# Marking the keys of the expert gates with three engines: squared distances on GpSimd, three second keys of sixteen on ScalarE

## What the reference computes

```python
s1, i1 = lax.top_k(s[:, :, 0], PEER_TOPK)
s2, i2 = lax.top_k(s[:, :, 1], PEER_TOPK)
cand_s = s1[..., :, None] + s2[..., None, :]
cand_i = i1[..., :, None] * N_KEYS + i2[..., None, :]
top_s, pos = lax.top_k(cand_s, PEER_TOPK)
idx = take_along_axis(cand_i, pos)            # 128 pairs for each token
gate = softmax(top_s)
act = gelu(einsum('pkd,pd->pk', expert_u[idx], t)) * gate
out = einsum('pk,pkd->pd', act, expert_v[idx])
```

## Time and profile before

| what | value |
|---|---|
| time, median of 3 runs | 5070.51 us (5069.15 to 5071.11) |
| profiled execution: its own time | 5068.12 us |
| its span, first to last instruction | 5066.4 us |
| TensorE / VectorE / ScalarE / GpSimd busy | 78% / 46% / 32% / 3% of the span |
| first scatter, 1339.3 to 1540.4 us | 201.1 us: TensorE 149.7, VectorE 179.9, ScalarE 181.8 busy |
| second scatter, 2991.0 to 3091.7 us | 100.7 us: TensorE 74.4, VectorE 90.0, ScalarE 90.9 busy |
| mean granted TensorE clock | 0.873 (1.0 is 2.4 GHz, 0.5 is 1.2 GHz) |

### The profile page before, as it was taken

How to read it: one execution, slowest core, us unless ns; L and a number is a source line. 1 busy time by engine, 2 the same in 40 slices (tenths; PEclk the granted TensorE clock), 3 DMA queues, 4 the chain that set the end, 5 groups by cost and what they waited for, 6 DMA issues and landing times. The chain is left out here.

```text
span 5066.4 us, 61125 instructions
## 1 busy us (share of the span) xinstructions
PE 3929.2 (78%) x20597; PEld 2743.7 (54%) x20597; DVE 2348.7 (46%) x4852; ACT 1609.3 (32%) x3013; POOL 170.8 (3%) x148
## 2 busy tenths in 40 slices
PE   5988998883376999999968635999846776677766
PEld 2448995342264787778745524999724532222223
DVE  0435662109985666666616296888534210000000
ACT  1223432111494444444314135666412111111111
POOL 0004430000000000000000000000000000000000
PEclk7979998996698999999989867999966878787888
DMA  7100001133065544455420207999420259999996
GB/s 264 66 0 1 1 1 67 42 122 111 6 193 174 186 175 166 173 185 180 146 70 34 75 0 249 345 318 317 168 107 34 75 249 427 426 427 427 426 427 286
DMA packets 302745, 904.97 MB, mean 179 GB/s; under 512 B 18672, under 2 KB 138736, under 8 KB 277104
## 3 DMA queue, kind: packets, MB, share of 16 engines
q1 hardware_dynamic: 302576, 902.68, 47.1%
HBM read 851.23 MB, written 51.38 MB: 178 GB/s over the span
## 5 line engine op out<-in xcount | busy, mean ns | idle before, releaser
L1595 PE MATMUL pd<-h_parts,u_parts 128*128 128x512 f32 x2048 | 485.4, 396 | 45.5 <-DVE u_parts L1681 45.5
L1608 PE MATMUL po<-act_parts,v_parts 128*128 128x512 f32 x2048 | 482.8, 393 | 9.9 <-DVE v_parts L1686 7.4
L283 PE MATMUL ps<-hT,w_stream 128*128 128x512 f32 (+1 forms) x1184 | 437.4, 533 | 47.6 <-ACTq L303 47.6
L1595 PEld LDWEIGHTS pd<-h_parts,u_parts 128*128 128x128 f32 x2048 | 384.9, 188 | 140.5 <-DVE u_parts L1681 45.7
L1608 PEld LDWEIGHTS po<-act_parts,v_parts 128*128 128x128 f32 x2048 | 383.7, 189 | 104.4 <-DVE v_parts L1686 21.7
L2710 PE MATMUL pb<-moe_ring,moe_xs 128*32 128x512 f32 x2048 | 331.1, 759 | 134.9 <-DMA moe_ring<-in_moe_gu 120.1
L283 PEld LDWEIGHTS ps<-hT,w_stream 128*128 128x128 f32 x1184 | 229.6, 194 | 256.2 <-issue 210.2
L2761 DVE TENSOR_TENSOR moe_hidden<-moe_silu,pg 128x512 f32<-128x512 f32 x16 | 11.0, 688 | 648.4 <-PE pg L2699 482.7
L1801 PE MATMUL pd<-h_parts,u_parts 128*128 128x256 f32 x2048 | 264.9, 283 | 43.0 <-DVE u_parts L1880 43.0
L1801 PEld LDWEIGHTS pd<-h_parts,u_parts 128*128 128x128 f32 x2048 | 261.6, 191 | 53.2 <-DVE u_parts L1880 43.2
L1423 PE MATMUL ps<-first_ind,second_ind 128*128 128x128 f32 x1536 | 224.2, 298 | 78.1 <-DVE second_ind L1409 37.8
(11 more groups left out here) (439 smaller groups left out, 6232.0 us busy)
## 6 DMA issues: line engine op xcount, KB each, us to landing
moe_ring<-in_moe_gu SPq DMA_DIRECT2D x128, 2048.0 KB, 26.4
u_stream<-in_peer_u SPq DMA_DIRECT2D x256, 512.0 KB, 6.2
v_stream<-in_peer_v SPq DMA_DIRECT2D x256, 512.0 KB, 4.9
moe_ring<-in_moe_down SPq DMA_DIRECT2D x64, 2048.0 KB, 26.5
ada_ring<-in_ada_w SPq DMA_DIRECT2D x24, 2048.0 KB, 15.7
peer_gates<-gate_stage SPq DMA_DIRECT2D x6, 8192.0 KB, 30.4
g_stream<-peer_gates SPq DMA_DIRECT2D x128, 256.0 KB, 5.0
w_stream<-in_gdn_w_in SPq DMA_DIRECT2D x8, 2048.0 KB, 8.2
```

Source lines behind the costliest of these rows:

```text
L283: mm = pe.matmul(ps[:, j, 0:T], wb[:, u, c, j * P:(j + 1) * P], hT[:, c, :], start=(c == 0), stop=(c == kc - 1))
L1595: m = pe.matmul(pd[:, j, 0:T], us[:, j, w, c], h[:, w, c], start=(c + w == 0), stop=(c == DC - 1 and w == 1))
L1608: m = pe.matmul(po[:, (c + b) % 4, 0:T], vs[:, j, w, (c + b) * P:(c + b) * P + P], aparts[:, 4 * half + j, w], start=(j + w == 0), stop=(j ...
```

## The change

The four engines share the marks in another way, and the loop over tiles is merged with that over turns except on ScalarE.

- GpSimd makes the squared distances of sets 0 and 2, each with two tensor_tensor instructions of 128x512: `first_off` = iota - first key, then `first_distance` = off x off, with a wait on the first before the second. ScalarE's eight squares go.
- ScalarE still makes `first_ind` of sets 0 and 2 by a relu of 128x512. It now makes `second_ind` of the last 3 tokens of 16 too: two small copies of the picks (second keys and gates, and gates with the sign turned), three squares, and three relus relu(gate - gate x d^2), with gate and -gate as per-partition bias and scale.
- VectorE makes 13 of the 16 `second_ind`, and `first_ind` of sets 1 and 3 as before, reading the first keys from `sel_T` directly.
- VectorE's slots come free with TensorE's product (`joined`), not with the evacuation (`taken`).
- The loops run through all tiles; ScalarE keeps its lead of one turn over tile borders.

The diff, cut to its added lines; the removed ones are those of the function printed above:

```diff
+    ALL = tiles * TURNS
+    OWN = 3
+    O0 = GROUP - OWN
...
+        off = k.sb(ctx, "first_off", [2, 4, P])
         dist = k.sb(ctx, "first_distance", [2, 4, P])
+        dist2 = k.sb(ctx, "second_distance", [OWN, P])
+        now = k.sb(ctx, "picks_now", [2, O0])
+        mine = k.sb(ctx, "picks_own", [3, OWN])
...
+        iota4 = C("iota").rearrange("p (a n) -> p a n", a=1).broadcast_to([P, 4, P])
+        def first4(at):
+            return selT[:, 0, bass.ds(at, 4)].rearrange("p (a n) -> p a n", n=1).broadcast_to([P, 4, P])
+        with nc.Block() as block:
+            @block.gpsimd
+            def _(pool):
+                with pool.Fori(0, ALL) as i:
+                    for x in range(2):
+                        pool.tensor_tensor(off[:, x], iota4, first4(i * GROUP + 8 * x), ALU.subtract).then_inc(by_pool.h, 1)
+                        pool.wait_ge(by_pool.h, by_pool.at(1 + 2 * x) + i * 4)
+                        pool.wait_ge(by_act.h, by_act.at(1 + x) + i * 3)
+                        pool.tensor_tensor(dist[:, x], off[:, x], off[:, x], ALU.mult).then_inc(by_pool.h, 1)
...
+                dve.sem_inc(by_dve.h, SETS)
+                with dve.Fori(0, ALL) as i:
+                    dve.wait_ge(by_dve.h, by_dve.at(SETS) + i * SETS)
+                    dve.tensor_copy(now[:], selT[:, 1:3, bass.ds(i * GROUP, O0)]).then_inc(picks.h, 1)
+                    dve.wait_ge(picks.h, picks.at(1) + i)
+                    for b in range(SETS):
+                        dve.wait_ge(joined.h, joined.at(1 + b) + i * SETS)
+                        if b % 2:
+                            dve.tensor_tensor(A[:, 4 * b:4 * b + 4], iota4, first4(i * GROUP + 4 * b), ALU.is_equal)
+                        for n in range(4 * b, min(4 * b + 4, O0)):
+                            m = dve.tensor_scalar(B[:, n], C("iota"), now[:, 0, n:n + 1], now[:, 1, n:n + 1], ALU.is_equal, ALU.mult)
+                        m.then_inc(by_dve.h, 1)
...
+                pe.sem_inc(joined.h, SETS)
+                with pe.Fori(0, ALL) as i:
+                    for b in range(SETS):
+                        if b % 2 == 0:
+                            pe.wait_ge(by_act.h, by_act.at(4 + b // 2) + i * 3)
+                        if b == SETS - 1:
+                            pe.wait_ge(by_act.h, by_act.at(6) + i * 3)
+                        pe.wait_ge(by_dve.h, by_dve.at(SETS + 1 + b) + i * SETS)
+                        pe.wait_ge(taken.h, taken.at(1 + b) + i * SETS)
...
+                act.sem_inc(by_act.h, 3)
+                def own_picks(i):
+                    act.wait_ge(by_act.h, by_act.at(3) + i * 3)
+                    act.activation(mine[:, 0:2], selT[:, 1:3, bass.ds(i * GROUP + O0, OWN)], ACT.Copy)
+                    act.activation(mine[:, 2], selT[:, 2, bass.ds(i * GROUP + O0, OWN)], ACT.Copy, scale=-1.0).then_inc(copied.h, 1)
+                def square(i):
+                    act.wait_ge(copied.h, copied.at(1) + i)
+                    for a in range(OWN):
+                        m = act.activation(dist2[:, a], C("iota"), ACT.Square, bias=mine[:, 0, a:a + 1], scale=-1.0)
                     m.then_inc(squared.h, 1)
+                def first(i, x):
+                    act.wait_ge(joined.h, joined.at(1 + 2 * x) + i * SETS)
+                    act.wait_ge(by_pool.h, by_pool.at(2 + 2 * x) + i * 4)
+                    act.activation(A[:, 8 * x:8 * x + 4], dist[:, x], ACT.Relu, bias=1.0, scale=-1.0).then_inc(by_act.h, 1)
+                def second(i):
+                    act.wait_ge(squared.h, squared.at(1) + i)
+                    act.wait_ge(joined.h, joined.at(SETS) + i * SETS)
+                    for a in range(OWN):
+                        m = act.activation(B[:, O0 + a], dist2[:, a], ACT.Relu, bias=mine[:, 1, a:a + 1], scale=mine[:, 2, a:a + 1])
+                    m.then_inc(by_act.h, 1)
+                def take(i, tile, at, b):
+                    act.wait_ge(joined.h, joined.at(SETS + 1 + b) + i * SETS)
+                    act.activation(stage[:, tile % 2, :, bass.ds(at + 4 * b, 4)], ps[:, b, :].rearrange("p (t n) -> p n t", t=4), ACT.Copy).then_inc(taken.h, 1)
...
+                own_picks(0)
+                square(0)
+                first(0, 0)
+                first(0, 1)
+                second(0)
                 for tile in range(tiles):
                     if tile >= 2:
                         act.wait_ge(written[tile % 2].h, written[tile % 2].at(DMA_DONE * (tile // 2)))
+                    last = tile == tiles - 1
+                    with act.Fori(0, TURNS - 1 if last else TURNS) as n:
+                        i = n + tile * TURNS
+                        at = n * GROUP
+                        own_picks(i + 1)
+                        take(i, tile, at, 0)
+                        first(i + 1, 0)
+                        take(i, tile, at, 1)
+                        square(i + 1)
+                        take(i, tile, at, 2)
+                        first(i + 1, 1)
+                        take(i, tile, at, 3)
+                        second(i + 1)
+                    if last:
+                        for b in range(SETS):
+                            take(ALL - 1, tile, P - GROUP, b)
```

More of the change, by code:

```diff
@@ L1378, in peer_scatter @@
     TURNS = P // GROUP
-    ind_b, joined, taken, squared = (k.sig(x) for x in ("sc_second", "sc_joined", "sc_taken", "sc_squared"))
-    picks, copied = k.sig("sc_picks"), k.sig("sc_copied")
-    ind_a = [k.sig("sc_first0"), k.sig("sc_first1")]
+    ALL = tiles * TURNS
+    OWN = 3
+    O0 = GROUP - OWN
+    by_pool, by_act, by_dve, picks, copied, squared, joined, taken = (
+        k.sig("sc_" + x) for x in ("by_pool", "by_act", "by_dve", "picks", "copied", "squared", "joined", "taken"))
     written = [k.sig("sc_written0"), k.sig("sc_written1")]
@@ L1384, in peer_scatter @@
         stage = k.sb(ctx, "gate_stage", [2, P, P])
+        off = k.sb(ctx, "first_off", [2, 4, P])
         dist = k.sb(ctx, "first_distance", [2, 4, P])
-        now = k.sb(ctx, "picks_now", [3, GROUP])
-        mine = k.sb(ctx, "first_now", [GROUP])
+        dist2 = k.sb(ctx, "second_distance", [OWN, P])
+        now = k.sb(ctx, "picks_now", [2, O0])
+        mine = k.sb(ctx, "picks_own", [3, OWN])
         A = k.sb(ctx, "first_ind", [GROUP, P])
         B = k.sb(ctx, "second_ind", [GROUP, P])
-        ps = k.banks(ctx, 4)
+        ps = k.banks(ctx, SETS)
@@ L1392, in _ @@
             @block.vector
             def _(dve):
[L1394 to L1411, removed]
@@ new lines, in _ @@
+                with pe.Fori(0, ALL) as i:
[6 more added lines that the diff above has]
+                        pe.wait_ge(taken.h, taken.at(1 + b) + i * SETS)
+                        for a in range(4):
+                            m = pe.matmul(ps[:, b, a * P:a * P + P], B[:, 4 * b + a], A[:, 4 * b + a], start=True, stop=True)
+                        m.then_inc(joined.h, 1)
@@ L1428, in _ @@
                 act.sem_inc(taken.h, SETS)
[L1429 to L1442, removed]
-                    m.then_inc(squared.h, 1)
@@ L1445, in indicate @@
[L1445 to L1451, removed]
@@ L1453, in _ @@
-                for tile in range(tiles):
[L1454 to L1459, removed]
+                act.sem_inc(by_act.h, 3)
[3 more added lines that the diff above has]
+                    act.activation(mine[:, 2], selT[:, 2, bass.ds(i * GROUP + O0, OWN)], ACT.Copy, scale=-1.0).then_inc(copied.h, 1)
@@ L1460, in _ @@
+                own_picks(0)
[3 more added lines that the diff above has]
+                second(0)
+                for tile in range(tiles):
                     if tile >= 2:
                         act.wait_ge(written[tile % 2].h, written[tile % 2].at(DMA_DONE * (tile // 2)))
[L1464 to L1473, removed]
@@ L1474, in _ @@
-                    with act.Fori(0, TURNS - 1) as i:
-                        turn_of(i, i * GROUP, False)
-                    turn_of(TURNS - 1, P - GROUP, True)
+                    last = tile == tiles - 1
[11 more added lines that the diff above has]
+                        second(i + 1)
@@ L1484, in _ @@
                     sp.wait_ge(w.h, w.at(DMA_DONE * tiles // 2))
[L1485 to L1493, removed]
+    by_pool.done(4 * ALL)
+    by_act.done(3 * ALL + 3)
+    by_dve.done(SETS * ALL + SETS)
+    for x in (picks, copied, squared):
+        x.done(ALL)
+    joined.done(SETS * ALL + SETS)
+    taken.done(SETS * ALL + SETS)
     for w in written:
```

## The result

The changed kernel takes 5156.34 us, median of four runs (5149.78 to 5158.40), against 5070.81 us before in the same comparison: a ratio of 1.0167, 95% interval 1.0154 to 1.0179. It is 85.5 us slower. The prediction had said 5195, which is 125 slower.

The account below looks back on a forecast made before the run. VectorE bounds the scatter: 5.10 us plus 3.82 of GpSimd collisions, 8.92, taken as 8.7 a turn against 5.87. Over 48 turns +136, less 11 at tiles, +125: 5195 us, 8 in 10 within 5085 to 5265.

Parts of the forecast that it names:

- The cause: Scatter: GpSimd and VectorE operations shut each other out until they end, one-input double-rate marks included; locked sum given 0.70.
- The doubt about the second scalar: VectorE's second-key marks: if the second per-partition scalar were free, 342 ns would fit the single rate as well.
- VectorE's own 5.10: VectorE's scatter turn without collisions: 5.87 us less three marks of 0.257 us, giving 5.10.
- The collisions, 3.82: Scatter turn: four GpSimd instructions hold up VectorE, 2 x (1.07 + 0.84) = 3.82 us added.
- ScalarE's 5.3: ScalarE's scatter turn after the change, summed from evacuations, relus, small operations and copies: 5.3 us.
- Tiles, -11: Tile borders and stage starts: refills saved, -12.8 us, against slower starts, +2; net -11.
- The 12.8 of the borders: Scatter tile borders: a refill of 3.2 us falls away at 3 + 1 borders, saving 12.8 us.
- The clock: TensorE in the scatter: granted clock may fall below 0.9; at 0.5 its work takes at most 9.4 us a turn.
- No exclusion (5032): Scatter rival: one-input operations not shut out, two-input ones meet a gap, ScalarE's 5.3 bounds; 5032 us, chance 0.10.
- VectorE keeping GpSimd out (5272): Scatter rival: GpSimd runs only when VectorE blocks on TensorE; turn 10.3 us, total 5272, chance 0.08.
- Only the tensor_tensor colliding (5094): Scatter rival: only VectorE's two first-key marks per turn collide with GpSimd; turn 6.6 us, total 5094, chance 0.12.
- the sign I gave: VectorE's first-key marks in the scatter were expected to last well above 685 ns.

## Why the prediction was right, point by point

**The time.** Measured 5156 for 5195: inside the range of 8 in 10, but just under the 5160 to 5225 that the prediction gave its own mechanism (a turn of 7.98, with 8.0 as the lower bound). The mechanism is right and the size is not.

**The cause.** Right, and shown from both sides: without GpSimd the marks are quick; with GpSimd and VectorE off the double rate, both are quick. A one-input operation at the double rate is shut out by GpSimd like a two-input one, which the trace of before could not show. The Trainium skill's rule ("SBUF — State Buffer", "Who interferes with whom") holds for tensor_scalar here: 1207 ns at most against a median of 341. The doubt about the second scalar is settled too: at one element at a time a mark takes 399 ns and is not held up, where it is 342 and held up otherwise. The 57 ns that the prediction gave the second scalar stand in no row; the rows leave it 342 - 227 - 65 = 50.

**VectorE's own 5.10.** Measured as 5.09 in the run without GpSimd, before ScalarE limits it, and as 5.15 by the line drawn back to no GpSimd.

**The collisions, 3.82, is the term that was mis-sized.** It measured 7.98 - 5.15 = 2.83 (2.89 from 5.09). The groups of the first scatter give the same: 13 x (529 - 342) + (566 - 182) ns = 2.8 us a turn (182 is the copy in the kernel with merged loops alone). Two parts of it: (a) I priced the square like line 1050, at 1.07, since it reads two whole rows; but it reads one tensor twice, takes 1.04 us and costs what the subtraction does, 2 x (1.07 - 0.84) = 0.46 less. Two different tensors cost 1.05, so the row was read rightly and applied wrongly. (b) Each instruction of 1.04 us costs VectorE 0.70 and not the 0.84 of a 904, 4 x 0.14 = 0.56 less. I had this among the lower bounds, as a mark's beginning that goes on while it waits and as GpSimd falling into VectorE's pauses; which share each has was not separated, but where a meeting is seen alone (the copy at 1425.24) 0.15 of the held instruction's 0.18 goes on inside the wait. My own correction for this was 0.2, and my turn 8.7. So (8.7 - 7.98) x 48 = 35 of the 40 us missing.

**ScalarE's 5.3** measured 5.55 in the run without GpSimd. The relus with two per-partition scalars take 491 ns against 394 for a square; I had allowed up to 0.1 each, and three of them make up the 0.25 missing.

**Tiles, -11.** The 12.8 of the borders measured 15.6 in the run that has only the merged loops. In the change itself the two scatters' +87 less 48 x (7.98 - 5.87) = 101 leave -14 for borders and starts together. That is 3 of the remaining 5 us; the rest is mostly that the medians differ by 85.5 and the profiled executions by 88.

**The clock.** It fell to 0.78 in the stage as thought and decided nothing: TensorE waits for marks, and ScalarE waits 70.6 us for TensorE while VectorE has no pause but for its copy.

**Rivals.** No exclusion (5032): its time came, 11 us off, only in the run without GpSimd. VectorE keeping GpSimd out (5272): GpSimd's subtraction has a mean of 1046 and its square 1125, against 1033 and 1039 at the shortest: it is let in behind the mark that runs. Only the tensor_tensor colliding (5094): this is what the run with the marks from PSUM is, at 5100; in the change itself they hardly met, and the sign I gave ("well above 685") was wrong at 697. So was the sign for the square, a mean above 1.27: it is 1.125. Which of VectorE's instructions is hit depends on when GpSimd is released, and GpSimd was released by ScalarE while marks ran.

## What to carry to other kernels

GpSimd is no free third hand beside a full VectorE: every instruction of it that was tried here held up VectorE's double-rate instructions (one input, two elements at a time), and those that read also its two-input ones. The price was two thirds of the length of an instruction of 1.04 or 0.52 us, and 1.05 of 1.26 for two tensors. Moved work must save VectorE more than that; here 2.83 us were paid to save 0.77. Before moving work to a new engine, look for a place in the same trace where the two already run side by side, compare the longest durations with the medians, and price each instruction from it. And look at what a full engine does between its instructions: two pauses of 0.33 and 0.22 us in a turn, ScalarE's wait for its own evacuation and a refill per tile were together worth 33 us, with no engine added.

## What the runs showed of the hardware that was not expected

- GpSimd's multiplication of a 128x512 float32 tensor by itself takes 1.04 us, of two tensors 1.26, with an operand repeated along the row 1.04. A fill takes 0.52; it shuts VectorE's second-key marks and its copy out too (0.33 us each), but not a first-key mark.
- When VectorE's marks are no longer held up, GpSimd's own instructions are: the subtraction went from 1046 to 1439 ns beside first-key marks, which took 1005 instead of 697.
- A ScalarE relu of 128x128 with scale and bias per partition takes 0.49 us, a square with bias alone 0.39.
- ScalarE's 5.70 us a turn before held waits that the trace showed as no idle time: with another wait in front of the squares it does the same work in 5.40. Twice 0.61 - 0.48 = 0.13 is most of it.
